# First loads in another layout, three lower parts by an adding DMA, and seven convolution taps moved

## Chip, cores and metric

The kernel runs on one core of one Trainium2 chip. The metric is the device time of one execution, in microseconds (us); less is better. TensorE (PE) multiplies, VectorE (DVE), ScalarE (ACT) and GpSimd (POOL) work elementwise, SyncE (SP) issues most DMAs.

## The reference

Two transformer blocks follow each other on x of 256 tokens by 1024 features, all in float32.

```
x = first_block(x, ...)    # rms_norm; h @ w_in (1024 x 8708); four kinds of attention; gates; w_out;
                           # rms_norm; relu(h @ w_up)^2 @ w_down; final rms_norm
x = second_block(x, ...)
def second_block(x, ...):
    h = rms_norm_2(x, norm1_g)
    q, k, v, u = split(h @ w_in)                       # 512, 512, 512, 1024 columns
    q, k = rope(rms_norm_2(q)), rope(rms_norm_2(k))    # 8 heads of 64
    attn = causal softmax attention(q, k, v)
    conv = silu(layer_norm(depthwise_conv31(a * sigmoid(g))))   # a, g = split(u + glu_b), 512 channels, 31 taps
    x = x + concat(attn, conv) @ w_out
    h = rms_norm_2(x, norm2_g)
    x = x + (silu(h @ w_gate) * (h @ w_up)) @ w_down
```

## The kernel before

**Products.** Float32 products are made of three passes in the faster type fp32r: each weight and each activation is split into a high part (its value rounded to fp32r) and a lower part (value minus high part), and PE adds hi*hi, lo*hi and hi*lo (lines 668 to 670). A group of `product` on a unit with four rows of 128 is twelve such matmuls of 512 columns for one half (128) of the tokens.

**Weights.** They come in units of 1 MB (128 partitions x 2048 floats), in the order in which PE uses them. SP loads unit i into `raw[i % 4]` (L560), and before it waits until unit i - 4 has been split, because that frees the buffer. ACT casts it to `whi[i % 4]` (`split_hi`, L1167) once PE is done with unit i - 4; DVE writes `wlo[i % 4] = raw - whi` (`split_lo`, L1636). PE waits for `s_lo` before the first group of a unit. Where on ACT and DVE a split stands between other work is set by `split_after`, by group number.

**Second input projection ("p2").** Five chunks i = 0 to 4 of 512 columns (u's two halves, then q, k, v) of two units each, called (i, 0) and (i, 1) here; the four groups of a chunk are stages 4i to 4i + 3, the first two on unit (i, 0), the last two on unit (i, 1). So stage 8 is the first that needs unit (2, 0), stage 12 unit (3, 0), stage 16 unit (4, 0). `timetable2` says what else is done beside which stage: `ut` and `rturn` turn tiles on PE (`rturn(2)` after stage 18), `ug` (L2155, L2159) makes the gated input of the convolution on DVE, `r0` (L2109), `ra` (L2128 to L2135) and `r1` (L2142, L2147) norm and rotate q and k on DVE, and `cv` does taps of the convolution (L2176, L2178). DVE does 62 taps (31 for each of two tiles of channels), the first 20 of them beside this projection and 42 in the attention that follows; the other two tiles of channels go over PE (L1005).

**Attention of the second block.** For 8 heads, in a pipeline: scores on PE (L1016, L1017), mask and maximum on DVE (`am`, L2192, L2194), exponential on ACT (L1508, L1509), turn on PE (L635), copy on ACT (L1515), product with V on PE (L1032 to L1034), scaled write on ACT (L1521, L1522). PE's part of the convolution (L1005) stands between these.

**POOL.** It has a program order of its own: powers for the norms (`root`, L2323), then four products `xr * par2` (L2365) whose results are needed after the attention, then the roots `q0` to `q3`.

**Start.** SP and ACT issue the first loads in pieces: unit 0 and unit 1 in pieces of 256 KB (one of 128 rows each), x transposed in five parts with rows of 1 KB, and a constant tile `cst` (identity and `g_mix`). `first_chunk` multiplies piece k of the first two units, k = 0 to 7, as they land.

Of the kernel before, what the change touches and what calls it, by code (L numbers as in the profile page):

```python
# [11 lines left out]
S = 256  # L12
# [16 lines left out]
def _layout():  # L29
    n = 0  # L30
    for name, w in (("g_mlp", 8), ("g_fin", 8), ("g_n1", 8), ("g_n2", 8), ("glu_b", 8),
                    ("dw_w", 124), ("dw_b", 4), ("ln_g", 4), ("ln_b", 4), ("b_f", 4), ("lam", 128),
                    ("g_diff", 64), ("dwb_ph", 4)):
        PAR[name] = (n, w)
        n += w
    PAR["_n"] = n
    n = 0
    for name, w in (("ident", 128), ("g_mix", 8), ("maskF", 256)):
# [145 lines left out]
def build(nc, ctx, x_d, xt_d, w_in, w_br, w_out, w_up, w_dn, w_in2, w_out2, w_g2, w_u2, w_gu, w_d2, par_d, par2_d, cst_d, tw_d, out_d):  # L184
# [66 lines left out]
    def sem(name):  # L251
        return ctx.enter_context(nc.semaphore(name))
# [3 lines left out]
    d_piece = [sem(f"d_piece{i}") for i in range(4 * NPC)]  # L256
    d_xt = [sem(f"d_xt{i}") for i in range(5)]
    d_cs0 = sem("d_cs0")
# [41 lines left out]
    ident = cst[:, 0:128]  # L300
    g_mix = cst[:, 128:136]
    maskF = cst[:, 136:392]

# [161 lines left out]
    x_v = x_d.rearrange("(t p) d -> p t d", p=128)  # L465
    xt_v = xt_d.rearrange("(k p) s -> p k s", p=128)
# [85 lines left out]
    def _(e):  # L552
        w = Gate(e)
        def load(i):
            v, kn, n = units[i]
            if i >= NRAW:
                w.wait_ge(s_hi, HALF[i - NRAW])
                w.wait_ge(s_lo, HALF[i - NRAW])
            dst = raw[:, i % NRAW, 0:kn * n].rearrange("p (k n) -> p k n", k=kn)
            e.dma_start(dst, v).then_inc(d_raw[i % NRAW], 16)  # L560

        def load_piece(i, k):
            v, kn, n = units[i]
# [27 lines left out]
        for i in range(NRAW, nu):  # L591
# [3 lines left out]
            if i == NRAW + 4:  # L595
                e.dma_start(cst[:, 136:N0], cst_d[:, 136:N0]).then_inc(d_cs1, 16)
                e.dma_start(cs1[:, 0:CST["MB"][0]], cst_d[:, N0:N0 + CST["MB"][0]]).then_inc(d_cs1, 16)
# [26 lines left out]
    def _(e):  # L624
# [21 lines left out]
        def product(tag, hi, lo, k0, t, bank_of, first, last, kr=None, at=None, cols=None, between=None):  # L646
# [6 lines left out]
            if i >= NPC:  # L653
                w.wait_ge(s_lo, HALF[i])
            krs = range(kn) if kr is None else kr
# [495 lines left out]
    def _(e):  # L1151
# [37 lines left out]

        e.dma_start(raw[:, 0, 256:512], units[0][0][:, 0, 256:512]).then_inc(d_piece[0], 16)  # L1190
        e.dma_start(cst[:, 0:136], cst_d[:, 0:136]).then_inc(d_cst, 16)

        e.preload_act_table_set("natural_log_exp_and_others")

        def input_hi(k):
            w.wait_ge(d_xt[XIN[k]], 16)
            e.mul(Ahi[:, k, :], xT[:, k, :], g_mix[:, k:k + 1]).then_inc(s_xh, 1)
# [4 lines left out]
        w.wait_ge(d_cst, 16)  # L1202
        for k in range(8):
# [418 lines left out]
    def _(e):  # L1622
# [49 lines left out]
        def input_lo(k):  # L1672
            w.wait_ge(s_xh, X["A", k, 0] + 1)
            e.scalar_tensor_tensor(out=Alo[:, k, :], in0=xT[:, k, :], scalar=g_mix[:, k:k + 1],
                                   in1=Ahi[:, k, :].bitcast(F32), op0=ALU.mult, op1=ALU.subtract).then_inc(s_xl, 1)

        w.wait_ge(d_piece[0], 32)
        e.tensor_copy(whi[:, 0, 0:512], raw[:, 0, 0:512]).then_inc(s_hi, 1)
        w.wait_ge(d_cst, 16)
        for k in range(8):  # L1680
# [634 lines left out]
    def _(e):  # L2315
# [157 lines left out]
```

## Time and profile before

| | |
|---|---|
| median of 3 runs | 770.51 us (769.64 to 770.77) |
| the profiled execution | 769.26 us, with a span of 767.1 us; some 2.2 us lie around the span |
| PE busy | 759.5 us, 99% of the span |
| DVE, ACT, POOL busy | 586.2, 408.7, 53.2 us |
| granted TensorE clock | 1.0 throughout |

A row of a timeline gives the start, the duration, the engine, the line of the kernel, the operation, what it writes and reads, and in brackets how long the engine sat idle before it and for whom it waited. Rows of merged instructions (x2, x4) give their number.

### The profile page before, as it was taken

Reading aid. Unit: us, or ns where it says so; the run is one execution under the profiler, and the core shown is the slowest. Engines: PE = TensorE matmul, PEld = TensorE weight load, DVE = VectorE, ACT = ScalarE, POOL = GpSimd, SP = SyncE. Lnnn points to the kernel's source line nnn. Section 1 sums busy time; section 2 is a strip of 40 time slices with the busy share of each in tenths; the row PEclk is TensorE's granted clock in tenths of the full one; section 3 lists DMA queues with packets and bytes.
Section 4 is the critical chain, followed back from the end, with each engine's and each line's share of the span. In section 5 each row is a group of like instructions: output and inputs, shape, how many; then the busy total and the mean of one; then the engine's idle time right before and its main releaser. Section 6 shows DMA issues by size and latency. Waiting matters only on the chain.

```text
span 767.1 us, 9650 instructions
## 1 busy us (share of the span) xinstructions
PE 759.5 (99%) x3712; PEld 636.5 (83%) x3712; DVE 586.2 (76%) x956; ACT 408.7 (53%) x552; POOL 53.2 (7%) x42
## 2 busy tenths in 40 slices
PE   8999999999999999999999999999999999999998
PEld 6888899888888888888888888888988888888886
DVE  5879798687757877787778838799767777768584
ACT  6765455465647546556554545864665445353430
POOL 0200000000002400000000002541000000000000
PEclk9999999999999999999999999999999999999999
DMA  9953444354345567555565557654133766555601
GB/s 317 389 199 101 147 138 165 123 200 146 137 164 165 165 216 253 189 203 193 191 218 172 180 197 275 219 177 161 56 111 109 236 203 199 185 194 190 213 7 55
DMA packets 68796, 137.28 MB, mean 179 GB/s; under 512 B 2576, under 2 KB 6544, under 8 KB 68240
## 3 DMA queue, kind: packets, MB, share of 16 engines
q1 hardware_dynamic: 68320, 135.44, 52.0%
q10 hardware_dynamic: 432, 1.25, 0.5%
q8 instruction: 29, 0.48, 0.3%
q14 instruction: 15, 0.12, 0.0%
HBM read 135.48 MB, written 1.05 MB: 178 GB/s over the span
## 4 chain that ended last, share of the span: by engine, by line
PE 90%; DVE 6%; ACT 3%; issue 1%; DMA 1%; SPq 0%; ACTq 0%
PE b L668 20%; PE b L670 20%; PE b L669 19%; PE SS L668 4%; PE SS L670 4%; PE SS L669 4%; PE TT L635 3%; PE OO L668 2%; PE OO L670 2%; PE OO L669 2%; DVE wlo L1636 2%; DVE ca L2178 2%; PE b L835 1%; PE SS L782 1%; ACT whi L1167 1%; PE OO L1005 1%
## 5 line engine op out<-in xcount | busy, mean ns | idle before, releaser
L1636 DVE TENSOR_TENSOR wlo<-raw,whi 128x2048 fp32r<-128x2048 f32 (+2 forms) x119 | 270.4, 2273 | 78.8 <-ACT whi L1167 78.0
L1167 ACT CAST whi<-raw 128x2048 fp32r<-128x2048 f32 (+2 forms) x119 | 223.2, 1880 | 123.9 <-PE b L670 81.8
L668 PE MATMUL b<-whi,Ahi 128*128 128x512 f32 (+2 forms) x520 | 206.3, 397 | 0.1
L670 PE MATMUL b<-whi,Alo 128*128 128x512 f32 (+2 forms) x520 | 199.8, 384 | 0.0
L669 PE MATMUL b<-wlo,Ahi 128*128 128x512 f32 (+2 forms) x520 | 199.1, 383 | 0.0
L670 PEld LDWEIGHTS b<-whi,Alo 128*128 128x128 f32 x520 | 97.6, 188 | 19.9
L669 PEld LDWEIGHTS b<-wlo,Ahi 128*128 128x128 f32 x520 | 97.9, 188 | 17.9
L668 PEld LDWEIGHTS b<-whi,Ahi 128*128 128x128 f32 x520 | 97.8, 188 | 17.9 <-ACT gates L1242 0.3
L2037 DVE STREAM_TRANSPOSE hT<-ust 32x256 f32<-32x256 f32 (+1 forms) x192 | 81.5, 424 | 2.8
L668 PE MATMUL b<-whi,Bhi 128*128 128x512 f32 x154 | 60.4, 392 | 0.1
L670 PE MATMUL b<-whi,Blo 128*128 128x512 f32 x154 | 60.0, 389 | 0.0
L669 PE MATMUL b<-wlo,Bhi 128*128 128x512 f32 x154 | 60.0, 389 | 0.0
L670 PE MATMUL SS<-whi,hlo 128*128 128x512 f32 x108 | 42.0, 389 | 0.0
L668 PE MATMUL SS<-whi,hhi 128*128 128x512 f32 x108 | 42.0, 389 | 0.0
L669 PE MATMUL SS<-wlo,hhi 128*128 128x512 f32 x108 | 42.0, 389 | 0.0
L2323 POOL TENSOR_TENSOR st<-st 128x2 f32<-128x2 f32 (+3 forms) x13 | 20.2, 1560 | 264.2 <-DVE st L1669 264.2
L668 PEld LDWEIGHTS b<-whi,Bhi 128*128 128x128 f32 x154 | 28.9, 188 | 6.3 <-ACT ust L1410 0.5
L670 PEld LDWEIGHTS b<-whi,Blo 128*128 128x128 f32 x154 | 28.9, 188 | 6.1
L669 PEld LDWEIGHTS b<-wlo,Bhi 128*128 128x128 f32 x154 | 28.9, 188 | 5.9
L1290 ACT ACTIVATE Sb<-Sb,st 128x384 f32<-128x384 f32 (+3 forms) x16 | 9.9, 619 | 38.3 <-DVE st L1818 38.3
L1753 DVE STREAM_TRANSPOSE qkA<-gates 32x128 f32<-32x128 f32 x80 | 24.2, 302 | 1.3
L1188 ACT CAST hhi<-hT 128x512 fp32r<-128x512 f32 (+1 forms) x24 | 13.3, 603 | 20.8 <-DVE hT L2037 20.8
(306 smaller groups left out, 1104.3 us busy)
## 6 DMA issues: line engine op xcount, KB each, us to landing
raw<-in_w_in SPq DMA_DIRECT2D x38, 1024.0 KB, 5.0
raw<-in_w_up SPq DMA_DIRECT2D x16, 1024.0 KB, 5.4
raw<-in_w_dn SPq DMA_DIRECT2D x16, 1024.0 KB, 5.0
raw<-in_w_d SPq DMA_DIRECT2D x11, 1024.0 KB, 4.9
raw<-in_w_g SPq DMA_DIRECT2D x10, 1024.0 KB, 5.0
raw<-in_w_u SPq DMA_DIRECT2D x10, 1024.0 KB, 5.0
raw<-in_w_out SPq DMA_DIRECT2D x8, 1024.0 KB, 5.1
raw<-in_w_br SPq DMA_DIRECT2D x4, 1024.0 KB, 5.0
```

The costliest lines, as they stand in the source:

```text
L635: ins = e.transpose(dst[:, 128 * k:128 * k + 128], src[:, 128 * k:128 * k + 128], ident)
L668: e.matmul(dst, xh, H[:, kc, c0:ce], start=first and kc == krs[0], stop=False)
L669: e.matmul(dst, xh, L[:, kc, c0:ce], start=False, stop=False)
L670: ins = e.matmul(dst, xl, H[:, kc, c0:ce], start=False, stop=last and kc == krs[-1])
L1167: e.copy(whi[:, s, 0:m], raw[:, r, 0:m]).then_inc(s_hi, 1)
L1188: e.copy(ph, src).then_inc(s_xh, 1)
L1290: ins = e.activation(P, P, ACT.Exp, bias=stat_m[i][:, 0:1], accum_out=stat_s[i][:, 0:1])
L1636: e.tensor_tensor(wlo[:, s, 0:m], raw[:, r, 0:m], whi[:, s, 0:m].bitcast(F32), ALU.subtract).then_inc(s_lo, 1)
L1753: ins = e.transpose(tile[:, :, :, 32 * k:32 * k + 32], src[32 * k:32 * k + 32, :, :, 32 * m:32 * m + 32])
L2037: ins = e.transpose(dst[32 * m:32 * m + 32, :, :, 32 * i:32 * i + 32], src[32 * i:32 * i + 32, :, :, 32 * m:32 * m + 32])
L2178: k_tap[k] = own(e.scalar_tensor_tensor(out=ca[:, k, :], in0=x, scalar=tap, in1=ca[:, k, :], op0=ALU.mult, op1=ALU.add))
L2323: e.tensor_tensor(r, v, mhalf[:, 0:n], ALU.pow).then_inc(s_rs, 1)
```

## The change

1. **First loads.** The transposed x is laid out in memory by partition, in four parts instead of five (k = 0, 1, 2 to 3, 4 to 7); `g_mix` comes with part 0, into `PT`. Part 0 is issued first on SP, then the first half of piece 0, then piece 1; part 1 is issued from ACT, in the place of the constants; the identity (64 KB) follows the pieces of unit 1. The two halves of piece 0 have a semaphore each and are cast by two DVE instructions.
2. **Three lower parts.** For units (2, 0), (3, 0) and (4, 0) (list `RD`) DVE makes no `wlo`. ACT writes `wlo = -whi` behind its cast, and POOL issues a DMA of 1 MB from `raw` into `wlo` that adds (`rest`). PE waits for that DMA's semaphore, and so does SP before it loads into the same `raw` buffer. On POOL, `rest(0)` and `rest(1)` stand between L2365 and root `q0`, and `rest(2)` between roots `q0` and `q1`.
3. **Taps.** At stages 10, 12, 14, 16, 18 DVE does 8, 4, 6, 5, 4 taps (27) in the place of 8, 2, 4, 3, 3 (20), and in the attention 35 in the place of 42.

```diff
-    for s, n in ((10, 8), (12, 2), (14, 4), (16, 3), (18, 3)):
+    for s, n in ((10, 8), (12, 4), (14, 6), (16, 5), (18, 4)):
         bg[s].append(("cv", n))
...
+    RD = [unit_of[tag] for tag in (('p2', 2, 0, 0), ('p2', 3, 0, 0), ('p2', 4, 0, 0))]
+    LOWS = [HALF[i] - sum(j <= i for j in RD) for i in range(nu)]
+    def lo_done(i):
+        return (d_rest[RD.index(i)], 16) if i in RD else (s_lo, LOWS[i])
...
-    XP = [(0, 1), (1, 2), (2, 4), (4, 6), (6, 8)]
+    XP = [(0, 1), (1, 2), (2, 4), (4, 8)]
...
                 w.wait_ge(s_hi, HALF[i - NRAW])
-                w.wait_ge(s_lo, HALF[i - NRAW])
+                w.wait_ge(*lo_done(i - NRAW))
...
+        load_xt(e, 0)
         e.dma_start(raw[:, 0, 0:256], units[0][0][:, 0, 0:256]).then_inc(d_piece[0], 16)
-        load_xt(0)
-        load_xt(1)
         load_piece(0, 1)
-        load_xt(2)
+        load_xt(e, 2)
         load_piece(0, 2)
         load_piece(0, 3)
-        load_xt(3)
+        load_xt(e, 3)
         load_piece(1, 0)
         load_piece(1, 1)
-        load_xt(4)
         load_piece(1, 2)
         load_piece(1, 3)
+        e.dma_start(cst[:, 0:128], cst_d[:, 0:128]).then_inc(d_cst, 16)
...
             e.copy(whi[:, s, 0:m], raw[:, r, 0:m]).then_inc(s_hi, 1)
+            if i in RD:
+                w.wait_ge(s_hi, HALF[i])
+                e.mul(wlo[:, s, 0:m], whi[:, s, 0:m].bitcast(F32), -1.0).then_inc(s_neg, 1)
...
-        e.dma_start(cst[:, 0:136], cst_d[:, 0:136]).then_inc(d_cst, 16)
+        load_xt(e, 1)
...
-                split_lo(i)
+                if i not in RD:
+                    split_lo(i)
...
-            conv(6 if k < 4 else 4 if k < 8 else 1)
+            conv(5 if k < 3 else 4 if k < 7 else 2 if k < 8 else 1)
...
+        def rest(k):
+            s, r, m = RD[k] % NSPL, RD[k] % NRAW, units[RD[k]][1] * units[RD[k]][2]
+            w.wait_ge(s_neg, k + 1)
+            e.dma_start(wlo[:, s, 0:m], raw[:, r, 0:m], accum_op=ALU.add).then_inc(d_rest[k], 16)
+
+        for k in range(len(RD) - 1):
+            rest(k)
         for i in range(4):
             root(f"q{i}", rpr[i], rpv[i], 8)
+            if i == 0:
+                rest(len(RD) - 1)
```

## Rows read from the trace of the kernel before

**Rows 1.** Two stretches: length, busy us of PE, PEld, DVE, ACT, POOL; clock; DMA.
```profile
470.00:526.00 56.00, 54.92 (x256) 45.19 (x255) 48.89 (x82) 35.77 (x52) 26.15 (x10) 1.00 0.60 212
526.00:560.00 34.00, 33.36 (x261) 31.25 (x259) 28.92 (x89) 18.42 (x61) 0.00 (x0) 1.00 0.28 94
```
**Rows 2.** Timeline of PE: stages 8 and 16 begin; turn after stage 18.
```profile
489.74 0.39 PE L668 MATMUL b<-whi,Ahi 128*128 128x512 f32 x1
...
513.28 0.48 PE L668 MATMUL b<-whi,Ahi 128*128 128x512 f32 x1
...
522.80 0.66 PE L635 MATMUL TT<-cst,PT 128*128 128x128 f32 x4 [1.08 <-DVE PT L2147]
```
**Rows 3.** Timeline of POOL: the four products, and root q0.
```profile
478.68 11.26 POOL L2365 TENSOR_TENSOR xr<-xr,par 128x512 f32<-128x512 f32 x4
501.50 3.61 POOL L2323 TENSOR_TENSOR st<-st 128x8 f32<-128x8 f32 x1 [11.56 <-DVE st L1669]
```
**Rows 4.** Timeline of DVE from 479 us.
```profile
479.91 2.28 DVE L1636 TENSOR_TENSOR wlo<-raw,whi 128x2048 fp32r<-128x2048 f32 x1
483.18 5.62 DVE L1636 TENSOR_TENSOR wlo<-raw,whi 128x2048 fp32r<-128x2048 f32 x2 [0.99 <-ACT whi L1167]
493.11 0.61 DVE L2155 SCALAR_TENSOR_TENSOR ch<-TT,par,ca 128x128 f32<-128x128 f32 x2 [4.31 <-PE TT L635]
...
498.16 2.46 DVE L2178 SCALAR_TENSOR_TENSOR ca<-ch,par,ca 128x256 f32<-128x256 f32 x6
500.53 0.68 DVE L2109 TENSOR_REDUCE st<-tg 128x8 f32<-128x512 f32 x1
...
501.33 2.28 DVE L1636 TENSOR_TENSOR wlo<-raw,whi 128x2048 fp32r<-128x2048 f32 x1
```
**Rows 5.** Timeline of ACT: casts of units (2, 0), (3, 0), (4, 0), then `r0`.
```profile
472.99 1.91 ACT L1167 CAST whi<-raw 128x2048 fp32r<-128x2048 f32 x1
...
483.61 1.92 ACT L1167 CAST whi<-raw 128x2048 fp32r<-128x2048 f32 x1 [0.47 <-PE OO L670]
...
495.91 1.91 ACT L1167 CAST whi<-raw 128x2048 fp32r<-128x2048 f32 x1 [0.20 <-PE b L670]
...
499.78 0.64 ACT L1490 ACTIVATE tg<-ust 128x512 f32<-128x512 f32 x1
```
**Rows 6.** DMA issues, 440 to 530 us: median from issue to landing.
```profile
raw<-in_w_in SPq DMA_DIRECT2D x8, 1024.0 KB, 5.1
...
hp<-odd SPq DMA_DIRECT2D x4, 35.8 KB, 1.9
```
**Rows 7.** SP's timeline: the load of unit (4, 0).
```profile
482.26 0.37 SPq L560 DMA_DIRECT2D raw<-in_w_in  x1
```
**Rows 8.** The page: what the DMA engines moved, in 40 equal slices.
```profile
GB/s 317 389 199 101 147 138 165 123 200 146 137 164 165 165 216 253 189 203 193 191 218 172 180 197 275 219 177 161 56 111 109 236 203 199 185 194 190 213 7 55
```
**Rows 9.** The chain that ended last, in the first 9 us.
```profile
2.12 4.29 DMA raw<-in_w_in
...
7.24 0.70 PE SS L686 x2
```
**Rows 10.** Timeline of ACT and PE: piece 4; then the cast of unit 4.
```profile
10.46 0.62 ACT L1175 CAST whi<-raw 128x512 fp32r<-128x512 f32 x1 [0.18 <-DMA raw<-in_w_in]
...
11.22 0.41 PEld L686 LDWEIGHTS SS<-whi,Ahi 128*128 128x128 f32 x2
...
24.43 1.91 ACT L1167 CAST whi<-raw 128x2048 fp32r<-128x2048 f32 x1 [1.13 <-DMA raw<-in_w_in]
```
**Rows 11.** Timeline of DVE and of PE: unit 4's lower part, and its first product.
```profile
26.38 2.29 DVE L1636 TENSOR_TENSOR wlo<-raw,whi 128x2048 fp32r<-128x2048 f32 x1 [1.84 <-ACT whi L1167]
...
28.81 0.47 PE L668 MATMUL b<-whi,Ahi 128*128 128x512 f32 x1
```
**Rows 12.** Timeline of PE near the end of the attention.
```profile
549.73 1.11 PE L1005 MATMUL OO<-hp,tw 128*128 128x128 f32 x8
550.92 0.41 PE L1032 MATMUL b<-V,PT 128*128 128x64 f32 x2
```

More of the change, by code:

```diff
@@ L37, in _layout @@
     n = 0
-    for name, w in (("ident", 128), ("g_mix", 8), ("maskF", 256)):
+    for name, w in (("ident", 128), ("maskF", 256)):
         CST[name] = (n, w)
@@ L256, in build @@
     d_piece = [sem(f"d_piece{i}") for i in range(4 * NPC)]
-    d_xt = [sem(f"d_xt{i}") for i in range(5)]
+    d_rest = [sem(f"d_rest{i}") for i in range(3)]
+    d_xt = [sem(f"d_xt{i}") for i in range(4)]
+    d_half = sem("d_half")
     d_cs0 = sem("d_cs0")
@@ L294, in build @@
     s_warm = sem("s_warm")
+    s_neg = sem("s_whi_negated")
+    s_half = sem("s_whi_half")
     def pcol(name, i=0, n=1):
@@ L300, in build @@
     ident = cst[:, 0:128]
-    g_mix = cst[:, 128:136]
-    maskF = cst[:, 136:392]
+    maskF = cst[:, 128:384]
+    g_mix, xT0 = PT[:, 0, 0:8], PT[:, 0, 8:264]
     def c1(name, a=0, n=None):
@@ L465, in build, with load_xt @@
     x_v = x_d.rearrange("(t p) d -> p t d", p=128)
-    xt_v = xt_d.rearrange("(k p) s -> p k s", p=128)
     xT = ys[:].rearrange("p t d -> p (t d)").rearrange("p (k s) -> p k s", k=8)
-    XP = [(0, 1), (1, 2), (2, 4), (4, 6), (6, 8)]
+    XP = [(0, 1), (1, 2), (2, 4), (4, 8)]
+    def load_xt(e, i):
+        a_, z_ = XP[i]
+        if i == 0:
+            e.dma_start(PT[:, 0, 0:264], xt_d[:, 0:264]).then_inc(d_xt[0], 16)
+        else:
+            e.dma_start(xT[:, a_:z_, :].rearrange("p k s -> p (k s)"),
+                        xt_d[:, 8 + S * a_:8 + S * z_]).then_inc(d_xt[i], 16)
     XIN = {k: i for i, (a, z_) in enumerate(XP) for k in range(a, z_)}
@@ L595, in _ @@
             if i == NRAW + 4:
-                e.dma_start(cst[:, 136:N0], cst_d[:, 136:N0]).then_inc(d_cs1, 16)
+                e.dma_start(cst[:, 128:N0], cst_d[:, 128:N0]).then_inc(d_cs1, 16)
                 e.dma_start(cs1[:, 0:CST["MB"][0]], cst_d[:, N0:N0 + CST["MB"][0]]).then_inc(d_cs1, 16)
@@ L653, in product @@
             if i >= NPC:
-                w.wait_ge(s_lo, HALF[i])
+                w.wait_ge(*lo_done(i))
             krs = range(kn) if kr is None else kr
@@ L683, in first_chunk @@
                 w.wait_ge(s_xh, X["A", k, 0] + 1)
+                if k == 0:
+                    w.wait_ge(s_half, 1)
                 w.wait_ge(s_hi, HALF[i] - 3 + kc)
@@ L1188, in x_hi @@
             e.copy(ph, src).then_inc(s_xh, 1)
-        e.dma_start(raw[:, 0, 256:512], units[0][0][:, 0, 256:512]).then_inc(d_piece[0], 16)
-        e.dma_start(cst[:, 0:136], cst_d[:, 0:136]).then_inc(d_cst, 16)
+        e.dma_start(raw[:, 0, 256:512], units[0][0][:, 0, 256:512]).then_inc(d_half, 16)
+        load_xt(e, 1)
         e.preload_act_table_set("natural_log_exp_and_others")
@@ L1196, in input_hi @@
             w.wait_ge(d_xt[XIN[k]], 16)
-            e.mul(Ahi[:, k, :], xT[:, k, :], g_mix[:, k:k + 1]).then_inc(s_xh, 1)
+            e.mul(Ahi[:, k, :], xT[:, k, :] if k else xT0, g_mix[:, k:k + 1]).then_inc(s_xh, 1)
         def input_square(t):
             e.activation(gates[:, t, 0:1024], xr[:, t, :], ACT.Square, accum_out=ss1[:, t:t + 1]).then_inc(s_sq, 1)
-        w.wait_ge(d_cst, 16)
         for k in range(8):
@@ L1673, in input_lo @@
             w.wait_ge(s_xh, X["A", k, 0] + 1)
-            e.scalar_tensor_tensor(out=Alo[:, k, :], in0=xT[:, k, :], scalar=g_mix[:, k:k + 1],
+            e.scalar_tensor_tensor(out=Alo[:, k, :], in0=xT[:, k, :] if k else xT0, scalar=g_mix[:, k:k + 1],
                                    in1=Ahi[:, k, :].bitcast(F32), op0=ALU.mult, op1=ALU.subtract).then_inc(s_xl, 1)
-        w.wait_ge(d_piece[0], 32)
-        e.tensor_copy(whi[:, 0, 0:512], raw[:, 0, 0:512]).then_inc(s_hi, 1)
-        w.wait_ge(d_cst, 16)
+        w.wait_ge(d_half, 16)
+        e.tensor_copy(whi[:, 0, 256:512], raw[:, 0, 256:512]).then_inc(s_half, 1)
+        w.wait_ge(d_piece[0], 16)
+        e.tensor_copy(whi[:, 0, 0:256], raw[:, 0, 0:256]).then_inc(s_hi, 1)
+        w.wait_ge(s_half, 1)
         for k in range(8):
@@ L2365, in _ @@
             e.tensor_tensor(xs, xs, par2[:, 512 * n:512 * n + 512], ALU.mult).then_inc(s_pg, 1)
+        def rest(k):
[4 more added lines that the diff above has]
+            rest(k)
         for i in range(4):
             root(f"q{i}", rpr[i], rpv[i], 8)
+            if i == 0:
+                rest(len(RD) - 1)
         for t in range(2):
@@ L2455 @@
     arrays = {
-        "x": a["x"][0], "xt": a["x"][0].T, "w_in": a["w_in"][0], "w_br": a["w_branch"][0].reshape(1024, 1024), "w_out": a["w_out"][0],
+        "x": a["x"][0], "xt": np.concatenate([col(a["mix_norm_g"], 8), a["x"][0].T.reshape(8, 128, 256).transpose(1, 0, 2).reshape(128, 2048)], axis=1), "w_in": a["w_in"][0], "w_br": a["w_branch"][0].reshape(1024, 1024), "w_out": a["w_out"][0],
         "w_up": a["w_up"][0], "w_dn": a["w_down"][0], "w_in2": a["w_in_2"][0], "w_out2": a["w_out_2"][0],
@@ L2460 @@
         "w_d2": a["w_down_2"][0],
-        "par": par, "par2": par2, "cst": np.concatenate([ident, col(a["mix_norm_g"], 8), tables], axis=1), "tw": _shifts(a["dw_w_2"][0]),
+        "par": par, "par2": par2, "cst": np.concatenate([ident, tables], axis=1), "tw": _shifts(a["dw_w_2"][0]),
     }
```

3 lines of the change are left out of this document (removed).

## The prediction, made before the result was known

> **What bounds the kernel now.** I read the busy time by stretch first. PE is at work nearly all the time, so the reader should look for the places where it is not, and for what would make new ones. In the second projection it is short of 1.08 us of 56, in the attention behind it of 0.64 us of 34, while DVE has 48.89 and 28.92 us in the same stretches [rows 1]. Then PE's timeline: the missing 1.08 us are one wait, before the turn after stage 18, and DVE's L2147 ends it [rows 2]. DVE's timeline says why. From 493.11, where it had been idle for 4.31 us until the turn after stage 8 gave it the first half of u, it has no idle time [rows 4] until past stage 18. So up to 493 DVE has room, and from there to 522.8 each added us on DVE is an us of PE. POOL's timeline has the third thing to see: the four L2365 took 11.26 us, from 478.68 to 489.94 [rows 3], and three DVE subtractions of 2.2 us each lie in that time, one at 479.91 and two from 483.18, and these two took 5.62 us and not 4.5 [rows 4]. 11.26 less three times 2.2 leaves 4.7: each of the two engines waits while the other has an instruction with two inputs in SBUF, and a product by itself takes 1.2 us.
>
> **First loads.** PE's run without holes begins at 7.24, after piece 1, which SP issued at 2.12 and which took 4.29 us [rows 9]. Piece 1 is now SP's third DMA and no longer its fourth: it goes out one issue earlier, some 0.4 us [rows 7], and 61 KB less stand before it (68 KB of constants out, 8 KB with part 0 in). That would be 0.5 us or a little more. But the pieces behind it must keep step. The cast of piece 4 began when its data landed, 10.46, and ended at 11.08, 0.14 us before PE's weight load of 11.22 [rows 10]. In the new order 512 KB of x stand before piece 4 in the place of 256: 195 KB more in all, at 389 GB/s [rows 8] 0.5 us, of which longer rows (4 and 2 KB for 1 KB) may give back 0.3. And further on unit 4's cast waits for its DMA at 24.43 [rows 10] and its lower part ends at 28.67, 0.14 us before PE takes it at 28.81 [rows 11]; the same bytes stand before that unit as ever. So the gain is cut to 0.14 us and whatever the queue as a whole gets faster. I take -0.2 us; bounds -0.6 (the whole step of piece 1 and a faster queue) and +0.4 (piece 4 late by 0.5).
>
> **Lower parts, first stall.** Unit (2, 0) is needed at 489.74 [rows 2]. Its subtraction was DVE's at 479.91, done at 482.2 [rows 4]. Now ACT's `-whi` is ready at 476.9 (cast from 472.99 [rows 5], then as long again, in a time when ACT had nothing to do until 480), but `rest(0)` stands behind L2365 on POOL. With the DVE subtraction at 479.91 gone, four products go at 1.2 us or a little more: 478.68 + 5.0 = 483.7, before the subtraction of unit (2, 1), which waits for ACT until 483.18. So the DMA is issued at 483.7, and PE is free of a stall only if it lands within 6.0 us.
>
> No row of before has an adding DMA. The nearest: a plain load of 1 MB lands 5.1 us after its issue, a small copy within SBUF after 1.9 [rows 6]. From below: 0.4 us of issue as on SP [rows 7] plus 5.1, landing at 489.2, no stall. The sum also reads the destination, another 1.05 MB, 2.7 us at 389 GB/s [rows 8]: 0.4 + 5.1 + 2.7 = 8.2 us. From above: two reads, the addition and the write one after the other, four times 2.7 us, plus 1.9 and 1 us of issue, 13.7 us. I take 8.2, since nothing lets the second read go for free: landing at 491.9, a stall of 2.2 us (bounds 0 and 7.7). Everything behind stage 8 moves along with it, DVE too, whose next work hangs on that turn.
>
> The Trainium skill, DMA: Bandwidth & Descriptors, Anatomy of one DMA (SWDGE path), has 2.0 us plus bytes over 436 GB/s for a DMA issued by GpSimd, an estimate of 4.4 us for this one: by that it would land at 488.1 and the stall be 0. Against that, Collectives: The Full Stack, The bandwidth ceiling, says that a reducing DMA is half as fast because it needs two source reads, not because of the addition; by an estimate from both pages it is 6.8 us and the stall 0.8. No row here shows either.
>
> `rest(1)`: ACT's cast of unit (3, 0) runs from 483.61 [rows 5], `-whi` follows to 487.4, landing about 495.6; stage 12 lies halfway between stages 8 and 16, at 501.5. No stall. ACT's sigmoids and evacuations behind it move by 1.9 us, but stage 8 and its turn come 2.2 us later too. The load of unit (4, 0), at 482.3 until now [rows 7], waits for `rest(0)`: 491.9 + 5.1 = 497.0, and with a stall of 2.2 us ACT can cast it only at 495.91 + 2.2 = 498.1 [rows 5]. Just covered; if `rest(1)` takes half of the queue, it is late by up to 2 us. The loads of (4, 1) and of the first unit of w_out queue behind it on SP and have over 4 us to spare.
>
> **Second stall, at stage 18.** (Times from here without the 2.2 us.) On DVE before r1(2): six taps more (2 each at 12, 14, 16), at 2.38 us for six [rows 4] +2.4; the subtraction of unit (4, 0) at 501.33 goes, -2.2. That would be +0.2. But ACT's cast of (4, 0) at 495.91 [rows 5] is now followed by a multiplication of 1.9 us, and queued behind that are the copies for the convolution's phases (until 499.15), the evacuation of stage 10 and `r0`'s square, 499.78 to 500.42 [rows 5]. DVE's L2109 took that at 500.53, with no time between [rows 4]; now it gets it at 502.4, and the room that the subtraction left is 1.9 us of idle time at exactly this place. The next square, of stage 11, ends at 505.3 on ACT against DVE's 505.54, so there DVE is 0.1 ahead and not 2.2; plus the taps, r1(2) is late by 2.2 us. PE's wait of 1.08 us [rows 2] grows to 3.3.
> `rest(2)` stands behind root q0. That root took 3.61 us at 501.50 beside the subtraction [rows 3], now some 1.7 from 503.3: issue at 505.0, landing 8.2 later at 513.2, up to 514 beside a load, for 513.28 [rows 2]. Up to 1 us of stall, which costs nothing, since PE waits for DVE two groups later anyway.
>
> **Attention.** DVE reaches it at +2.5 and has seven taps less (0.397 each, -2.8), so ends at about -0.3. That buys little: PE's own work is the bound. Adding what lies between the starts of its groups beyond their usual distance (as 1.19 us for 0.89 at 549.73 [rows 12]), I find 1.7 us of holes in 30 from 526.5 to 556.8, and 1.0 of these lie after 549, in the tail of heads 6 and 7 over ACT. 0.3 can be won.
>
> **Sum.** -0.2 + 2.2 + 2.2 - 0.3 = +3.9 us. On the profiled execution's 769.26 us that is 773.2; the median of the runs is 1.25 above it, so 774.4.
>
> **Rivals.**
> - *The adding DMA is much slower* (11 us and over, near the upper bound). Stall at stage 8 of 5 to 7.7 us; `rest(1)` still fits, as stage 12 moves along; `rest(2)` at 505 + 13 against 513.3 is 4.7 late, 2.5 beyond what DVE's wait covers. +7 to +11: 777.5 to 781.5. For it: 16 DMA engines add nothing in this trace, so none of this is measured. 0.20.
> - *Hidden and even.* It lands in 6 us, ACT's multiplication falls in gaps, the taps cost 0.2: total within 1.5 us, 769 to 772. For it: only 2.2 us separate 8.2 from 6.0; against: DVE has no gap after 493. 0.14. The 4.4 us from the Trainium skill's DMA page would lead here.
> - *Faster: the attention is bound by DVE's taps.* There the chain goes from DVE's maximum over ACT to PE, and DVE is busy without a break to 551. With `rest(0)` in time and r1(2) not later than 522.7, 2.8 us less on DVE would win all 1.7 us of PE's holes, and the start up to 0.6: 768.2. It decides where r1(2) lies: if that is late by more than 1.7 us, this is lost. The 0.64 us missing of 34 [rows 1] speak against it. 0.13.
> - *The forecast*, both stalls, +1.5 to +7: 0.53.
>
> **How the numbers follow.** No change is within 0.2%, 1.5 us, about what a measurement of this kernel tells. Below 770.0 lie the faster rival and a little of the even one; above 780 the slowest adding DMAs, together under 2 in 10; the range is 770.0 to 780.0. Slower: 0.53 + 0.20 = 0.73; same 0.14; faster 0.13.
>
> **What would show it.** The first matmul of the unbroken run at 6.7 to 7.1 and stage 1 of the first projection hardly earlier than now; POOL's four L2365 in 5 us; from the issue of `rest(0)` to PE's first matmul of stage 8 some 8 us, with PE idle for 2.2; DVE idle for nearly 2 us before L2109; PE's wait for L2147 about 3.3 us; a shorter DVE end in the attention with PE's length hardly changed. The prediction is wrong if the adding DMA takes 6 us or less, or 11 or more, if POOL spends long on issuing it and so holds up root q0, or if DVE does not go idle at 500.6.

## The result: 783.1 us, 12.6 slower, where 3.9 were forecast

The changed kernel takes 783.11 us (median of 6 runs, 782.79 to 783.84) and the kernel before 770.53 (6 runs on the same chip, 769.64 to 770.77): ratio 1.0166, 95% interval 1.0153 to 1.0179. The sign was forecast, the time lies outside the range. The two profiled spans differ by 13.8 us (780.9 for 767.1), 1.2 more than the medians, since the profiled execution of the kernel before was one of its fastest (769.26 us). How far the same matmul of the two PE timelines lies behind tells where:

| place | forecast | found in the trace |
|---|---|---|
| start of the first projection | -0.2 | +1.36 |
| matmuls on Bhi, Blo, hhi, hlo, 231 to 486 us | none | +4.93 |
| second projection, stage 8 | +2.2 | +1.15 |
| second projection, stages 16 to 18 | +2.2 | +4.84 |
| attention | -0.3 | -0.47 |
| from there to the end, mostly matmuls on the same tiles | none | +1.98 |
| sum | +3.9 | +13.8 |

**The start.** PE's timeline of the kernel after, from the end of the warming matmuls (a row of x2 holds two matmuls, the first number is its start):

```profile
2.76 1.48 PE L714 MATMUL OO<-Blo 128*128 128x512 f32 x3
5.46 1.19 PE L701 MATMUL SS<-whi,Ahi 128*128 128x512 f32 x2 [1.22 <-DVE whi L1698]
6.45 1.05 PE L704 MATMUL SS<-whi,Alo 128*128 128x512 f32 x2
7.30 1.05 PE L707 MATMUL SS<-wlo,Ahi 128*128 128x512 f32 x2
8.15 1.05 PE L701 MATMUL SS<-whi,Ahi 128*128 128x512 f32 x2
```

The same place in the kernel before:

```profile
4.71 0.94 PE L686 MATMUL SS<-whi,Ahi 128*128 128x512 f32 x2 [0.47 <-ACT Ahi L1197]
5.49 0.63 PE L689 MATMUL SS<-whi,Alo 128*128 128x512 f32 x2
```

PE waits 1.22 us for the first half of whi, and then the pairs start 0.85 us apart; from 9.75 on it is 0.45, as in all that follows. That is half pace, 0.43 us for one matmul, the same as behind the wait at stage 16, further down, where the granted clock is 0.50 (1.2 GHz). The granted clock in the row of this stretch (third column from the end) reads 1.00, and that must not be taken for a measurement:

```profile
5.40:9.70 4.30, 4.24 (x10) 3.40 (x11) 3.75 (x8) 3.17 (x6) 0.00 (x0) 1.00 1.03 391
```

The trace's record of the granted clock has its first entry, 1.00 (2.4 GHz), only at 9.60 us, and the row counts time without an entry as 1.00. The matmuls reach full pace at 9.75. In the kernel before the first entry is at 5.17 (so its "1.0 throughout" holds from there on) and the matmuls are at 0.24 us from 5.25. That the clock was the lower one (1.2 GHz) before the entry is read from the spacing.

Piece 1 did come earlier, as forecast, but the first product came later, and the pairs behind it run at half pace for 4 us. How much of the +1.36 is the change's is told further down, by other executions of the old loads. The chain in the same stretch names what it waits for, the first half of piece 0, 3.80 us under way:

```profile
1.19 3.80 DMA raw<-in_w_in
...
5.02 0.30 DVE whi L1698
...
5.46 1.19 PE SS L701 x2
```

**The products on the moved tiles.** The groups of PE by line, of the kernel before (L669) and after (L682); between the two bars stand busy us and mean ns of one:

```profile
L669 PE MATMUL b<-wlo,Ahi 128*128 128x512 f32 (+2 forms) x520 | 199.1, 383 | 0.0
L669 PE MATMUL b<-wlo,Bhi 128*128 128x512 f32 x154 | 60.0, 389 | 0.0
L669 PE MATMUL SS<-wlo,hhi 128*128 128x512 f32 x108 | 42.0, 389 | 0.0
```

```profile
L682 PE MATMUL b<-wlo,Ahi 128*128 128x512 f32 (+2 forms) x520 | 199.7, 384 | 0.0
L682 PE MATMUL b<-wlo,Bhi 128*128 128x512 f32 x154 | 60.8, 395 | 0.0
L682 PE MATMUL SS<-wlo,hhi 128*128 128x512 f32 x108 | 42.7, 395 | 0.0
```

Six ns are easily overlooked, but 1,224 matmuls of 512 columns in the kernel have Bhi, Blo, hhi or hlo as the stationary operand, and PE is hardly ever idle there. From start to start they stand 0.2333 us apart in the kernel after; in before those on hhi stand 0.2266 apart and those on Bhi 0.2273. Ahi's did not change. The diff has no word about these products. But the tile of constants, `cst`, lost its eight columns of `g_mix`, and each tile allocated behind it now lies 32 bytes lower. Ahi lies ahead of it. The trace can't prove that this is the cause; the experiments can.

**The second projection.** The two stretches of [rows 1]:

```profile
470.00:526.00 56.00, 51.08 (x237) 41.77 (x237) 37.53 (x72) 42.76 (x57) 15.92 (x12) 0.99 0.82 247
526.00:560.00 34.00, 33.57 (x225) 30.41 (x224) 33.17 (x89) 15.39 (x49) 5.15 (x2) 0.96 0.54 186
```

PE lacks 4.9 of 56 us, for 1.08. POOL's timeline, against [rows 3]:

```profile
484.89 5.04 POOL L2385 TENSOR_TENSOR xr<-xr,par 128x512 f32<-128x512 f32 x4
489.87 1.03 POOL L2390 DMA_DIRECT2D wlo<-raw  x1
494.08 0.87 POOL L2390 DMA_DIRECT2D wlo<-raw  x1 [3.18 <-ACT wlo L1185]
513.53 2.04 POOL L2343 TENSOR_TENSOR st<-st 128x8 f32<-128x8 f32 x1 [18.58 <-DVE st L1687]
515.53 0.90 POOL L2390 DMA_DIRECT2D wlo<-raw  x1
```

The four products take 5.04 us and no longer 11.26, as forecast. The chain from there on, and then PE's timeline where stages 8 and 16 begin, the rows that answer to [rows 2]:

```profile
489.87 7.12 DMA wlo<-raw
...
497.05 9.01 DMA raw<-in_w_in
...
506.09 1.92 ACT whi L1182
...
508.03 1.92 ACT wlo L1185
```

```profile
497.04 0.50 PE L681 MATMUL b<-whi,Ahi 128*128 128x512 f32 x1 [0.84 <-DMA wlo<-raw]
...
525.05 0.77 PE L681 MATMUL b<-whi,Ahi 128*128 128x512 f32 x1 [4.08 <-DMA wlo<-raw]
525.62 0.63 PE L682 MATMUL b<-wlo,Ahi 128*128 128x512 f32 x1
526.05 0.63 PE L683 MATMUL b<-whi,Alo 128*128 128x512 f32 x1
```

```profile
535.09 0.66 PE L648 MATMUL TT<-cst,PT 128*128 128x128 f32 x4
```

The first addition takes 7.12 us and makes PE wait 0.84. The load of unit (4, 0) starts only when it has landed and then takes 9.01 us; the usual one takes 5.1 [rows 6]. What the DMA engines did from its issue, 497.05, to 501.8:

```profile
q0 software_dynamic: 111, 0.91, 114.2%
...
raw<-in_w_in SPq DMA_DIRECT2D x2, 1024.0 KB, 10.1
```

POOL's queue q0 moved 111 packets and SP's queue q1, which has no line, none, though two loads were issued: the engines were full with the second addition, and the first packet of a load moved at 501.83. The two did not share, one waited for the other. ACT casts the unit with a wait for that load, makes `-whi`, and only then comes to the evacuation and to `r0`, for which DVE is idle 4.49 us at L2129. Root q0 and the third addition behind it are late by that, the addition takes over 9 us (its own first packet moves 2.8 us after the issue, at 518.29, when those of a load of w_out are nearly through), and PE waits 4.08 us at stage 16. The turn after stage 18 (the last fence) has no wait left. DMA issues from 475 to 520 us, and then the granted clock around the wait at stage 16 (third column from the end):

```profile
raw<-in_w_in SPq DMA_DIRECT2D x4, 1024.0 KB, 8.9
wlo<-raw POOLq DMA_DIRECT2D x3, 1024.0 KB, 9.4
```

```profile
524.00:526.00 2.00, 0.94 (x2) 0.83 (x3) 1.97 (x5) 1.24 (x2) 0.47 (x1) 0.75 0.00 0
526.00:528.00 2.00, 2.00 (x6) 1.57 (x5) 2.00 (x2) 0.00 (x0) 2.00 (x1) 0.50 0.92 248
528.00:530.00 2.00, 2.00 (x9) 1.61 (x9) 1.97 (x5) 0.00 (x0) 1.14 (x1) 0.89 1.05 406
```

The wait costs more than itself: behind it the clock is 0.50 (1.2 GHz; the record has it from 525.01 to 528.42), and matmuls start 0.43 us apart and not 0.23 until 528.53. Eight starts from 525.05 take 3.48 us for 1.84, 1.6 us more. The wait, this, and less the 1.08 that went at stage 18: 4.6 of the 4.84.

### The profile page after: what moved, and what is told of

Read it like the earlier page. It is cut to its first block, busy times and chain, and to the rows that moved or that the text cites. A ratio compares the mean times of both kernels' runs of the same rounds, so it can differ in the third digit from the quotient of the medians.

```text
span 780.9 us, 9651 instructions
## 1 busy us (share of the span) xinstructions
PE 769.4 (99%) x3712; PEld 638.8 (82%) x3712; DVE 579.9 (74%) x954; ACT 413.2 (53%) x555; POOL 48.1 (6%) x45
## 3 DMA queue, kind: packets, MB, share of 16 engines
HBM read 135.48 MB, written 1.05 MB: 175 GB/s over the span
## 4 chain that ended last, share of the span: by engine, by line
PE 87%; DVE 6%; ACT 3%; DMA 3%; POOL 1%; issue 1%; SPq 0%; ACTq 0%; POOLq 0%
PE b L681 19%; PE b L683 19%; PE b L682 19%; PE SS L681 4%; PE SS L682 4%; PE SS L683 4%; PE TT L648 2%; PE OO L681 2%; PE OO L682 2%; PE OO L683 2%; DMA raw<-in_w_in 2%; DVE wlo L1653 2%; PE OO L1020 1%; PE b L850 1%; PE SS L797 1%; DVE ca L2198 1%
## 5 line engine op out<-in xcount | busy, mean ns | idle before, releaser
L1653 DVE TENSOR_TENSOR wlo<-raw,whi 128x2048 fp32r<-128x2048 f32 (+2 forms) x116 | 262.6, 2266 | 86.0 <-ACT whi L1182 85.3
L682 PE MATMUL b<-wlo,Ahi 128*128 128x512 f32 (+2 forms) x520 | 199.7, 384 | 0.0
L682 PEld LDWEIGHTS b<-wlo,Ahi 128*128 128x128 f32 x520 | 98.4, 189 | 17.8
L682 PE MATMUL b<-wlo,Bhi 128*128 128x512 f32 x154 | 60.8, 395 | 0.0
L682 PE MATMUL SS<-wlo,hhi 128*128 128x512 f32 x108 | 42.7, 395 | 0.0
L682 PEld LDWEIGHTS b<-wlo,Bhi 128*128 128x128 f32 x154 | 28.9, 188 | 6.8
L681 PEld LDWEIGHTS SS<-whi,hhi 128*128 128x128 f32 x108 | 20.2, 187 | 5.0
```

Of the source, the lines that this page charges most:

```text
L681: e.matmul(dst, xh, H[:, kc, c0:ce], start=first and kc == krs[0], stop=False)
L682: e.matmul(dst, xh, L[:, kc, c0:ce], start=False, stop=False)
L1653: e.tensor_tensor(wlo[:, s, 0:m], raw[:, r, 0:m], whi[:, s, 0:m].bitcast(F32), ALU.subtract).then_inc(s_lo, 1)
```

## The experiments

All were compared with the kernel before on the same chip, 770.0 to 770.3 us.

### Is it the eight columns?

`e1_after_padded` is the kernel after, `e2_before_shifted` the kernel before, each with one line changed:

```diff
-    cst = sb("cst", [128, N0])
+    cst = sb("cst", [128, N0 + 8])
```

> The changed kernel with the tile cst 8 columns (32 bytes) wider, unused. Theory (addresses): the change took 8 columns out of cst, so every tile behind it starts 32 bytes lower, Bhi, Blo, hhi and hlo at 32 modulo 64, and each of the 1224 matmuls that take their stationary operand from them comes 6 to 7 ns later after the one before (0.2333 for 0.2267 us). With the columns back: 783.1 - 1224 x 0.0066 = 775 us, matmul rows on Bhi and hhi at 389 ns again. Rival (something else slows these matmuls, for instance the traffic of the other DMA queue or the clock): 783 us, rows at 395 ns.

> The kernel before with the tile cst 8 columns wider and nothing else, so that Bhi, Blo, hhi, hlo start at 32 modulo 64. Addresses: 770.5 + 8.1 = 778.6 us, rows on Bhi and hhi at 395 ns, rows on Ahi unchanged. Rival: 770.5, no row changed.

e1 took 776.4 us, 6.7 less than the kernel after (ratio to before 1.0076, 1.0058 to 1.0095), with Bhi and hhi back at 389 ns. e2 took 776.87 (1.0085, 1.0070 to 1.0100), 6.6 more than before, Bhi and hhi at 395. So eight unused columns, which no instruction touches, bring or take over half of the loss. That was my theory. What about the address counts was not yet known, and my first two ideas on it fell:

> The kernel before with cst 16 columns (64 bytes) wider: the tiles behind it are moved too, but stay at a multiple of 64. Theory (addresses modulo 64): 770.5 us, rows on Bhi and hhi at 389 ns. Rival (any move of them costs, or a boundary wider than 64 bytes matters): 778 us, or something between, rows above 389 ns.

> The kernel before with 32 unused columns (128 bytes for each partition) more in the tile of constants, so that every tile behind it lies 128 bytes further; no instruction is changed. In the kernel before the tiles whose matmuls became slower (Bhi, Blo, hhi, hlo) start at multiples of 128 bytes, and moves of 32 and of 64 bytes cost 6.6 and 6.9 us. Theory: what counts is that the stationary operand starts at a multiple of 128 bytes, so this move costs nothing: 770.3 us, within 1 us, and the rows of Bhi and hhi at 389 to 392 ns. Rival: any move of these tiles against the others costs it (a bank, or the distance to the moving operand): 777, rows at 395 to 398.

With `N0 + 16` (64 bytes) it took 777.12 us (1.0087, 1.0072 to 1.0101). With `N0 + 32` (128 bytes) 775.73 (1.0072, 1.0055 to 1.0089). The groups by line of the run with 128 bytes:

```profile
L669 PE MATMUL b<-wlo,Ahi 128*128 128x512 f32 (+2 forms) x520 | 199.1, 383 | 0.0
L669 PE MATMUL b<-wlo,Bhi 128*128 128x512 f32 x154 | 60.8, 395 | 0.0
L669 PE MATMUL SS<-wlo,hhi 128*128 128x512 f32 x108 | 42.7, 395 | 0.0
```

Neither 64 nor 128 bytes is the unit. Laying out the tiles by their sizes shows that in before all of them, moving (whi, wlo) and stationary, start at the same place of a stretch of 512 bytes. Four runs told the size of the stretch, and the address from the distance. f2 has `N0 + 64` (256 bytes). f3 and f4 put an unused tile of 32 bytes ahead of `raw`, and ahead of `Ahi`:

```diff
+    spare = sb("spare", [128, 8])
     raw = sb("raw", [128, NRAW, 2048])
...
+    spare = sb("spare", [128, 8])
     Ahi = sb("Ahi", [128, 8, S], F32R)
```

f5 allocates `st`, 1,536 bytes, ahead of `raw` and not behind `cst`.

> The kernel before with 64 unused columns (256 bytes for each partition) more in the tile of constants. In before every tile of matmul operands starts at 128 modulo 512 bytes, and a slice of the stationary operand is 512 bytes long. Theory: what counts is where in a stretch of 512 bytes the slice starts, so this move costs like the others: 776 to 777, Bhi and hhi at 395 ns. Rival: the stretch is 256 bytes: 770.3, rows at 389.

> The kernel before with 32 unused bytes ahead of all tiles, so that the moving operands (whi, wlo) and all stationary ones (Ahi, Alo, Bhi, Blo, hhi, hlo) move together and no distance between them changes. Theory 1, the distance between the stationary and the moving operand counts: 770.3, all rows as before. Theory 2, the address of the stationary operand itself counts: all of its matmuls are slower, also the 1,740 of Ahi and Alo (0.0066 us each, 11.5 us, beside the 6.6 of the others): 786 to 789, rows of Ahi at 395 too.

> The kernel before with 32 unused bytes between xr and Ahi: the moving operands stay, all stationary ones move by 32 bytes. Theory: Ahi and Alo are like Bhi and hhi, and their 1,740 matmuls of 512 columns start 0.0066 us further apart too: 786 to 789. Rival: Ahi and Alo are not touched by it (something other than the operand of these matmuls is slow, in the stages of Bhi and hhi): 777.

> The kernel before with the tile of statistics (1,536 bytes) ahead of the raw weights and not behind the constants: moving operands, Ahi, Alo, ys and constants lie 1,536 bytes higher, which is 0 modulo 512 and 512 modulo 1,024; Bhi, Blo, hhi and hlo stay. Theory, 512 bytes count (address or distance): 770.3, all rows as before. Rival, 1,024 or more count: Bhi and hhi against the moving operand, or Ahi, at 395, and 777 or more.

| run | moved against whi and wlo | us | ratio, interval |
|---|---|---|---|
| e2 | Bhi to hlo by 32 bytes | 776.87 | 1.0085 (1.0070 to 1.0100) |
| e6 | by 64 | 777.12 | 1.0087 (1.0072 to 1.0101) |
| e8 | by 128 | 775.73 | 1.0072 (1.0055 to 1.0089) |
| f2 | by 256 | 770.48 | 1.0004 (0.9994 to 1.0013) |
| f5 | by -1,536 | 770.44 | 1.0002 (0.9993 to 1.0012) |
| f3 | nothing; all tiles moved by 32 | 770.38 | 1.0003 (0.9994 to 1.0012) |
| f4 | all stationary tiles by 32 | 784.19 | 1.0182 (1.0165 to 1.0199) |

The rows of f4:

```profile
L670 PE MATMUL b<-wlo,Ahi 128*128 128x512 f32 (+2 forms) x520 | 201.8, 388 | 0.0
L670 PE MATMUL b<-wlo,Bhi 128*128 128x512 f32 x154 | 60.9, 395 | 0.0
L670 PE MATMUL SS<-wlo,hhi 128*128 128x512 f32 x108 | 42.7, 396 | 0.0
```

f3 decides: the addresses of all operands are as odd there as in e2, and nothing is lost. It is the distance of the stationary from the moving operand, and f2 says modulo 256 bytes. (The tiles `raw` and `xr` kept their places beside whi and wlo in every run, so a distance from one of them would look the same; that it is the moving operand's is the plain reading, and no run parts them.) My guess for f2, 512, was wrong. f4 shows that Ahi and Alo are like the others (starts 0.2331 us apart for 0.2280): 0.0051 us on each of their 1,632 matmuls of 512 columns is 8.3 us, which with the 6.6 of e2 makes 14.9; 14.2 were measured. I had expected more, since I took 0.0066 for all.

The Trainium skill, SBUF — State Buffer, Operand start alignment, asks only that an operand start at a multiple of its element's size, and says of this "This is about legality, not speed". The tiles of every run above satisfy it, and the times lie up to 14 us apart.

### The start

`e3_start_alone` is the kernel before with the first loads of the change and the old addresses (no adding DMA, old taps). `e7_start_warmer` adds, and `e9_before_warmer` has by itself, with the loads as before:

```diff
-        for i in range(6):
+        for i in range(8):
             e.matmul(bank[7], Blo[:, 0, 0:128], Blo[:, 0:2, :], start=True, stop=True)
```

> The first part of the change alone (first loads), addresses kept by 8 unused columns in cst. Theory (cold TensorE): the first products wait until 5.46, 1.2 us after the last warming matmul, and the first nine or ten pairs then run at half pace (0.85 us a pair for 0.45), which costs more than the earlier piece 1 gives: 770.5 + 1.3 = 771.8 us. Rival (forecast, loads set the start): 770.3 us, -0.2.

> The first part alone as before, addresses kept, with eight warming matmuls in the place of six, which end at about 5.1. Theory (cold TensorE): no pause of over half a microsecond before the first product, full pace from there: the unbroken run then depends on the loads alone and ends the first chunk at about 16.8 in the place of 18.4: 770.3 us. Rival (pace at the start has another cause, the loads): 771.8 us as without them.

> The kernel before with 8 matmuls of nothing ahead of the first product in the place of 6; loads as before. It tells what of the 1.2 us that two more of them brought with the new loads belongs to them alone. Theory: the new loads are worth nothing by themselves, and the runs of before differ by 1.7 us only because some of them start at the lower clock; then this is 769.2, with a narrow spread, as low as with the new loads. Rival: before starts at the full clock anyway, its PE has no gap there, and two more matmuls delay the first product by up to 0.7 us: 770.3 to 771.

e3 took 770.89 us (1.0008, 0.9999 to 1.0018; its runs spread from 768.77 to 771.32). e7 took 769.0 (0.9985, 0.9977 to 0.9994; 768.77 to 769.51). e9 took 769.17 (0.9988, 0.9979 to 0.9996; 768.93 to 769.43). PE's timeline of e7:

```profile
2.76 2.33 PE L714 MATMUL OO<-Blo 128*128 128x512 f32 x5
5.48 1.19 PE L701 MATMUL SS<-whi,Ahi 128*128 128x512 f32 x2 [0.39 <-DVE whi L1698]
6.47 0.91 PE L704 MATMUL SS<-whi,Alo 128*128 128x512 f32 x2
7.22 0.62 PE L707 MATMUL SS<-wlo,Ahi 128*128 128x512 f32 x2
```

The first product starts when it does in the kernel after, 5.48 for 5.46. But PE idles 0.39 us and not 1.22 before it, and full pace comes at 7.2 and not at 9.7; the last pair of the first chunk starts at 16.74 us for 17.95. With the loads as before, two more warming matmuls give the same time. So the loads by partition are worth nothing measurable, and what the start can win lies in the pace of its first products.

The runs of before and of e3 spread over 2 us, those of e7 and e9 over 0.75 or less, and the traces tell why. The first entry of the granted clock, 1.00, stands at:

| loads, warming matmuls | traces | first entry, us |
|---|---|---|
| old, 6 | before, e4, f5 | 5.17, 4.41, 4.14 |
| old, 6 | e2, e5, e6, e8, e10, e11, f2, f3, f4 | 8.98 to 10.79 |
| new, 6 | after, e1, e3 | 9.60, 9.67, 10.64 |
| 8 | e7 (new), e9 (old), e12 (new) | 7.10, 7.28, 6.24 |

f3 and f5 have the instructions of the kernel before and lose nothing to their addresses:

```profile
4.81 1.22 PE L687 MATMUL SS<-whi,Ahi 128*128 128x512 f32 x2 [0.57 <-ACT Ahi L1198]
```

```profile
4.88 0.73 PE L686 MATMUL SS<-whi,Ahi 128*128 128x512 f32 x2 [0.64 <-ACT Ahi L1197]
```

f3 (the upper line) has its entry at 10.61, f5 at 4.14; at the matmul of 231 us f3 is 1.25 us behind f5, and its span is 1.3 us longer (768.6 for 767.3). So with six warming matmuls some executions have full pace from the start and most do not, and the times of these two, 769.5 and 770.73, differ by as much. With eight the entry is never that early and never that late in three traces (though e12, also with eight, has two of its twelve runs at 771.04, of which there is no trace). The idle time does not decide it alone: it was 0.57 in f3 and 0.64 in f5. It also puts the +1.36 of the first table in its place: at that matmul f2 is 1.22 and f3 1.48 us behind the trace of the kernel before, with the old loads. The trace of before is one of the quick starts, and the changed kernel starts like most traced executions of the old one. The other rows of that table add up to 12.4 of the 12.6 us between the medians. By the medians the new loads cost 0.6 us (e3), with an interval that holds 0.

### The adding DMAs

`e4_adding_dma_alone` is the kernel before with this part only, and two variants of it: in `e10_first_addition_early` POOL issues the first addition ahead of its four products, and in `e11_two_additions` DVE subtracts unit (3, 0) as ever (the edit against e4):

```diff
-    RD = [unit_of[tag] for tag in (('p2', 2, 0, 0), ('p2', 3, 0, 0), ('p2', 4, 0, 0))]
+    RD = [unit_of[tag] for tag in (('p2', 2, 0, 0), ('p2', 4, 0, 0))]
```

> The second part alone: three lower parts by the adding DMA, taps and start as before. Theory (DMA queue): the first lands 7.2 us after its issue, PE waits 1.0 at stage 8; the load of unit (4, 0) shares the queue with the second and takes 9 us, so that the third DMA is issued late and PE waits some 4 us at stage 16, at half clock for 2 us behind it: 770.5 + 1.1 + 4.8 = 776.4 us. Rival (DVE's lateness at stage 18 as forecast, with taps the larger part): without the six taps 770.5 + 2.2 = 772.7 us.

> The kernel before with the adding DMAs alone (775.8 us), but the first of them is issued ahead of GpSimd's four products of the final norm and not behind them: at about 477.4 in the place of 484.1. Theory: the stall at stage 8 goes (landing at 484.5 to 486, needed near 489.7), the load of unit (4, 0) starts some 6 us earlier and no longer lies wholly beside the second addition, ACT casts it without its wait of 2.9, DVE's idle time before its square of stage 10 shrinks from over 4 us to 2 or less, the third addition is issued 2 to 3 us earlier and the wait at stage 16 falls from 4.3 to at most 1.5: 771 to 773 in all. Rival: the third addition hangs on GpSimd's root alone and takes over 9 us whenever it is issued: only the stall of stage 8 goes, 774.5 to 775.

> The kernel before with the adding DMAs alone, but for units (2, 0) and (4, 0) only; unit (3, 0) is subtracted by DVE as before. Theory: the second addition is what makes the load of unit (4, 0) take 9 us. Without it the load takes 5 to 6, ACT casts unit (4, 0) 3 us earlier, and the last addition is issued earlier and lands before or at most 1.5 us after PE wants it, against 4.3: 772 to 774 with the stall of stage 8 unchanged. Rival: the load is slow because of other loads, and stays at 9 us; the 4.3 us wait stays, and DVE has 2.2 us more to do: 775.5 to 777.

e4: 775.84 us (1.0072, 1.0054 to 1.0091). e10: 774.56 (1.0063, 1.0050 to 1.0076). e11: 771.5 (1.0019, 1.0010 to 1.0028). PE's waits of e4, of e10 and of e11 from 470 to 530 us (sum, times, longest):

```profile
PE b L676 <- DMA wlo<-raw: 5.3, 2, 4.3
```

```profile
PE b L676 <- DMA wlo<-raw: 3.8, 2, 3.5
```

```profile
PE b L676 <- DMA wlo<-raw: 2.4, 2, 1.3
```

e10 went the way of its rival. Its trace runs 1.16 us behind e4's here, since the start. POOL's root before the products ends only at 480.3, so the addition goes out 5.0 us earlier and not 6.7, and the chain shows what became of that:

```profile
480.26 11.45 DMA wlo<-raw
...
491.77 8.47 DMA raw<-in_w_in
```

It goes out behind a plain load, whose packets move from 480.86 to 485.41; its own first one moves at 484.67. It takes 11.45 us in the place of 7.16 and lands 0.7 us earlier, not 5. The load behind it still waits for the packets of the second addition: issued at 491.77, its first one moves at 496.77. e11 took the second addition away, and the same load took 5.15 us (492.02 to 497.17), ACT no longer waits for it, the third addition was issued at 507.75 and not at 509.75, and the wait at stage 16 fell from 4.3 to 1.1. That is my theory, with a time 0.5 us below its range, and the rival (775.5 to 777) is out. The first addition's stall stays in it.

### The taps

> The third part alone: seven taps from the attention to the projection. Forecast's view: DVE reaches L2147 six taps (2.4 us) later, PE waits 3.5 us there for 1.1, and 0.3 to 0.5 us come back in the attention: 770.5 + 2.0 = 772.5 us. Rival (the attention is bound by DVE's taps): up to 1.7 us come back, 771.2 us or less.

> The change turned round: the kernel before with the new first loads, 8 warming matmuls in the place of 6 and the old addresses (together 769.0), and three taps fewer, not seven more, under the second projection: one fewer at stage 16, two at stage 18, and three more in the attention. Theory: PE's wait of 1.08 us after stage 18 for DVE goes, since DVE gets there 1.2 us earlier, and the attention, where DVE has three taps (1.2 us) more, is bound by PE with room for them: 768.1. Rival: the chain from DVE's maximum over ACT to PE is lengthened by the taps and takes it all back: 769.0 to 769.6.

e5 is the kernel before with the new counts of taps alone. It took 773.36 us (1.0040, 1.0026 to 1.0054). Its wait after stage 18, and that of e12:

```profile
PE TT L635 <- DVE PT L2147: 3.4, 1, 3.4
```

```profile
PE TT L648 <- DVE PT L2167: 0.7, 1, 0.7
```

The wait in e5 is the 1.08 of before and the 2.4 of six taps, to 0.1 us. The turns of its trace are 0.78 us late at 483 us, from a start at the lower pace, 3.14 at stage 18 and 2.67 at the end of the attention: the taps cost 2.4 and give back 0.5. That leaves 1.2 of the 3.1 us of the median that are not the taps'. Three of its six runs took 771.6 to 772.4 us, the profiled one among them, and three 774.3 to 774.6; what set these three apart is not shown, and at 2.5 us it is more than the starts in the traces of the old loads differ by (1.8). e12 is e7 with the change turned round:

```diff
-    for s, n in ((10, 8), (12, 2), (14, 4), (16, 3), (18, 3)):
+    for s, n in ((10, 8), (12, 2), (14, 4), (16, 2), (18, 1)):
...
-            conv(6 if k < 4 else 4 if k < 8 else 1)
+            conv(7 if k < 3 else 6 if k < 4 else 4 if k < 8 else 1)
```

It took 769.29 us (0.9993, 0.9985 to 1.0002), no better than e7's 769.0. In its trace the turn after stage 18 comes 0.65 us earlier than in e7's, at 522.24 for 522.89. Of that 0.25 stand there since the start; the taps' part is 0.4, the wait of 0.7 for 1.1. The attention takes all 0.65 back by 551.7, in part in waits for ACT's L1539 of 0.8 us in all for 0.4. So seven taps fewer win 0.5 us there and three more cost 0.65: each way what one stretch gains the other gives back, wholly or in part. Best of all that ran are e7 and e9, 0.15% and 0.12% below the kernel before; their intervals overlap.

## Why the prediction was wrong, point by point

**No term for the addresses.** This is the step that failed most: my sum had no term for the products outside the parts that the diff speaks of, and 6.7 of the 12.6 us lie there (e1). I had listed the 68 KB of constants as bytes that a transfer no longer carries, and not asked what stands behind a tile that shrinks. I could have seen that the tiles move, but no row of before shows the price.

**First loads, "-0.2 us".** Neither borne out nor refuted: +0.6 by e3, with an interval that holds 0, and -0.2 by e7 against e9, within their intervals. The working was incomplete. I followed piece 1 in the queue; what ended the first wait became the half of piece 0 whose landing I took as unchanged, and I gave no thought to the pace of the first products. (A slip beside it: the eight columns of `g_mix` are 4 KB with part 0 and not 8; that is worth 0.01 us.)

**First stall, "+2.2".** The issue was right to 0.1 us: with the two earlier terms (6.3 us) taken off, 489.87 is 483.6 for 483.7. The products were right, 5.04 us for 5.0. The duration was mis-sized: 7.12 us and not 8.2, so the stall was 0.84 and the loss 1.15 us. The 5.1 of [rows 6] run from the start of the issue, so the 0.4 was counted twice, and what the addition has over a plain load was 2.0 us and not 2.7 (in e11, 2.4: 1.6 to its first packet for 1.0, and packets for 5.35 us for 3.5, against the plain load issued at 525.02 in before). The two estimates made from the Trainium skill's pages were 4.4 and 6.8 us; the run lies nearer to the second, that of Collectives: The Full Stack, The bandwidth ceiling, by which a reducing DMA is half as fast.

**"Just covered; if `rest(1)` takes half of the queue, it is late by up to 2 us."** This sentence named the mechanism that decided, and I gave it no term. It did not take half of the queue but all of it: the load's packets began only when the second addition's were nearly through. The load took 9.01 us, ACT waited 2.93 us for it, and e11 shows that the second addition was the reason.

**"DVE idle for nearly 2 us before L2109."** The place was right, 4.49 us the size: the 1.9 of ACT's multiplication and the late load together.

**"Up to 1 us of stall, which costs nothing, since PE waits for DVE two groups later anyway."** Turned round, and the second step that failed: the forecast had 2.2 us for this stage, by DVE's lateness, and nothing for `rest(2)`; the trace has 4.84, by `rest(2)` and the clock behind its wait. The third addition took 9.4 us and not 8.2, and was issued later for the reason above; PE waited 4.08 us for it and 1.6 more went with the clock behind the wait. It was DVE's wait for r1(2) that was covered. Therefore the parts do not add: e4 and e5 cost 5.6 and 3.1 by themselves, the start 0.6 and the addresses 6.6, together 15.9 us, and the change 12.6.

**The taps** were right: 3.4 us for the 3.5 that follow without the other parts, and the attention at -0.47 for -0.3.

**The rivals.** The one of 777.5 to 781.5 had the right stage, the right wait (`rest(2)`) and nearly its size (4.7 late), but for a duration of 11 us or more for every addition. Only additions beside other transfers came near to that (9.4, and 11.45 in e10). Without the addresses the change would have taken 776.4, inside my range and outside the forecast's 774.4 by 2.0.

## What to carry to other kernels

When an edit changes the size of a tile, look at what is allocated behind it, and compare the mean time of the same matmul before and after, by tile: 6 ns of 389 are 6.6 us here. The stationary tile should lie a multiple of 256 bytes from the moving one. A large DMA put in the place of work on an engine also slows the loads that fly beside it: cost it with its neighbours and theirs with it (7.1 us alone, 9.4 behind a load; the load 9.0 for 5.1), and follow what waits for the slowed load. Last, compare starts by more than one trace: here two executions of the same instructions (f3, f5) lie 1.25 us apart from the start on, and two more warming matmuls, worth 1.05 us (e9), did more than the new loads.

## What the runs showed of the hardware that was not expected

- Matmuls with a moving operand of 512 columns in fp32r start 0.2266 to 0.228 us apart on average, and 0.2333 where the stationary operand's distance from the moving one is 32 or 64 bytes off a multiple of 256 (0.2325 at 128 bytes). The absolute address does not matter (f3). Why is not shown.
- A DMA from SBUF to SBUF with addition, 1 MB, takes 7.1 to 7.5 us with little beside it and 8.2 to 11.45 beside a load or another addition; POOL is busy 0.9 to 1.0 us with each issue. A plain load issued while its packets move takes 8.5 to 9.0 us for 5.1: its own packets came after the addition's (first one 4.8 us after the issue).
- With six warming matmuls the granted clock's first entry came at 4.1 to 5.2 us in three traces and at 9.0 to 10.8 in twelve, with eight at 6.2 to 7.3 in three; in the fifteen traces with an entry after 6 us the matmuls start 0.43 us apart or more ahead of it and reach 0.23 within 0.25 us behind it. A row of a stretch without an entry reads 1.00. At stage 16 the idle time of 4.08 us was followed by a granted clock of 0.50 for 3.4 us.
